# Splitting two weight blocks on VectorE, keeping key roots in PSUM, and spreading the gate columns over the last memory head

## The chip, the cores and the metric

The kernel is one program on one core of one Trainium2 chip. The metric is the device time of one execution in microseconds: a median of 1459.05 us over 3 runs (1458.96 to 1459.29). The profile shows another execution of the same program. Its engines are called PE (TensorE), DVE (VectorE), ACT (ScalarE), POOL (GpSimd) and SP (SyncE).

## The reference, cut to what matters

A two-layer encoder trunk with 512 tokens, width 1024 and a memory of 256 rows. Everything in this document happens in the first 8% of it: the keys and values that both layers read from the memory, the normed input of the first layer, and 16 "gate" columns (beta and decay of 8 heads) of the first layer's input projection.

```python
mem_n = rms_norm(mem, mem_norm[i])                 # once per layer i
mk, mv = jnp.split(mem_n @ w_mem_kv[i], 2, axis=-1)
k = rms_norm(mk.reshape(B, M, 4, 128), k_norm)     # 4 memory heads per layer
v = mv.reshape(B, M, 4, 128)
...
h = rms_norm(x, norm)
proj = h @ w_in                                    # q, k, v, z and, 8 columns each, b and a
beta = jax.nn.sigmoid(b)
g = -jnp.exp(a_log) * jax.nn.softplus(a + dt_bias)
```

After that come the gated delta rule over 8 heads, memory attention, output projection and feed-forward layer, then a second layer with sliding-window attention. None of that is touched.

## The kernel before, in words

**Precision.** Every large product is made of three: weights and activations are each split into a rounded part (`hi`) and the rest (`lo`), and PE sums hi x hi, hi x lo and lo x hi. A weight block is 128 rows by 1024 columns, that is eight 128x128 tiles, so one block is 24 matmuls.

**The weight stream.** SP loads blocks into a ring of four (`w_raw`), ACT rounds each (`upper`, writes `w_hi`, counts `hi_done`), POOL subtracts (`lower`, L563, writes `w_lo`, counts `lo_done`), and PE waits for `lo_done` before a block's first matmul (`product`, L621). SP loads block b when blocks up to b-4 have been split; ACT rounds block b when PE has used block b-4.

**Order.** Each engine runs its own fixed list, in the order in which the code is written; semaphores are the only ties. So what an engine waits for holds up everything that stands behind it in its list.

**Start.** The memory rows are scaled on ACT, transposed on PE (L641, two k-tiles share one PSUM bank), and split by ACT (`mem_upper`) and DVE (`mem_lower`), which takes four buffers' turns with it. In ACT's list the rounding of weight blocks 0 and 1 stands ahead of `mem_upper(0)`.

**Memory projections** (`mem_proj` on PE, `mem_keys` on ACT, `mem_kv` on DVE; layer 0, then layer 1). A head takes a value block and a key block, 24 matmuls of 128x256 each. DVE copies both from PSUM; PE transposes the values (L673) and sums the squared keys (`key_sums`, L651, into bank D[4]); ACT makes the root as Ln and Exp (`key_rstd`), which in the kernel before is written to the SBUF tile `w(KRS)`; DVE multiplies keys, gain and root into `kmem` (`key_normed`). The key sums of a head stand on PE after the next head's value block, those of the last head at the end.

**The input.** Between the layers PE transposes x (L683, 32 transposes for 8 k-tiles, four banks in turn) and DVE copies it to `xT`. During layer 1, `norm_rows` (L699) spreads the root of each row, and DVE and ACT make the normed tiles between the heads: `x_normed` (DVE, PSUM), `x_upper` (ACT), `x_lower` (DVE), in three banks in turn. `X_TILES` says beside which head a tile stands: 0 and 1 after the first head's keys, then one before and one after the keys of heads 1 and 2, and 6 and 7 before the keys of head 3.

**Gate columns** (L709). After layer 1, 24 matmuls of 16 columns by 512 make `ba_raw`. Then `proj_dn(0, j)`, j = 0 to 3, are the first four blocks of the input projection, with the gate chain between them: transposes (L882), exp and log on ACT, three memsets and four column copies on DVE, `conv_tile(0, 0)` (DVE adds three shifted taps, which frees the PSUM bank of block j = 0), cumulative sums (L888, L889), row matmuls (L897).

The bank names: `D = [2, 3, 4, 5, 6, 7]`.

Of the kernel before, what the change touches and what calls it, by code (L numbers as in the profile page):

```python
# [126 lines left out]
def yoco_kernel(nc, x, mem, w_stream, w_out, w_down, w_ba, cols_in, squares_in, dist_in, out):  # L127
    with ExitStack() as ctx:
# [206 lines left out]
        def w(i):  # L335
            return ws[:, i, :]
# [221 lines left out]
        def _(pool):  # L558
# [32 lines left out]
            lower_all("mem0", 8)  # L591
# [20 lines left out]
        def _(pe):  # L612
# [41 lines left out]
            def mem_proj(layer, beside=None):  # L654
                b0, n0 = BLOCK0[f"mem{layer}"], TILE0[f"mem{layer}"]
                pe.wait_ge(S.m_evac_lo, KT * (layer + 1))
                for j in range(MEM_HEADS):
# [20 lines left out]
            mem_proj(0)


            def x_transposes(k):
                for t in range(NT):
                    mm = nc.tensor.transpose(bank[:, D[k % 4], t * P:(t + 1) * P],  # L683
                                             ws[:, 2 * t:2 * t + 2, :].rearrange("p a c -> p (a c)")[
                                                 :, k * P:(k + 1) * P], sq(IDENT))
                return mm
            pe.wait_ge(S.x_loaded, 16)
            pe.wait_ge(S.m_evac_lo, 2 * KT)
# [18 lines left out]
            for k in range(KT):  # L707
                for m, (wi, at) in enumerate(((0, act_hi), (0, act_lo), (1, act_hi))):
                    mm = nc.tensor.matmul(bank[0:16, D[3], :], ba_w[:, wi, k * 16:(k + 1) * 16], at[:, k, :],  # L709
                                          start=(k == 0 and m == 0), stop=(k == KT - 1 and m == 2))  # L710
            mm.then_inc(S.ba_raw, 1)
# [536 lines left out]
        def _(act):  # L1248
# [34 lines left out]
            upper(0, 0)  # L1283
            upper(0, 1)
# [420 lines left out]
        def _(dve):  # L1705
# [546 lines left out]
```

## Time and profile before

| | |
|---|---|
| median of 3 runs | 1459.05 us (1458.96 to 1459.29) |
| the profiled execution | 1458.45 us, of which 1456.7 us are the span |
| PE busy | 1421.3 us (98% of the span), 9400 matmuls |
| PE weight loads | 1146.4 us (79%) |
| DVE, ACT, POOL busy | 38%, 40%, 38% |
| DMA | 124.15 MB, 85 GB/s mean |
| granted TensorE clock | 0.998 mean |

A row of the timeline has the start in us from the span's start, the duration in us, the engine, the line, the operation with output and inputs, the shape, how many instructions are merged, and in brackets how long the engine was idle before it and on whom it waited. Matmuls overlap: a matmul row of 0.28 us may be followed 0.12 us later by the next, so distances between starts are what counts.

### The profile page before, as it was taken

The page shows a single profiled execution, that of the slowest core. Times are in us where ns is not written, and L with a number is a line of the kernel's source. Part 1 is how long each engine was busy: PE and PEld are TensorE (multiplying, and loading weights), DVE is VectorE, ACT ScalarE, POOL GpSimd, SP SyncE. Part 2 cuts the span into 40 slices and gives each one's busy share as a digit, 9 for nine tenths or more (in the row PEclk, how much of TensorE's full clock was granted, in tenths as well). Part 3 has the DMA queues.
Part 4 walks back from the last instruction along what each step waited for, and adds up shares of the span by engine and source line. Part 5 has one row for each costly group of instructions (what it writes and reads, how often), then busy time and mean ns, then how long its engine had stood idle before and what let it go on. Part 6 is the DMA issues. An engine that isn't in the chain of part 4 may idle for free.

```text
span 1456.7 us, 24342 instructions
## 1 busy us (share of the span) xinstructions
PE 1421.3 (98%) x9400; PEld 1146.4 (79%) x9400; DVE 559.7 (38%) x1054; ACT 578.8 (40%) x989; POOL 555.0 (38%) x270
## 2 busy tenths in 40 slices
PE   6989999999999999999999999999999999999998
PEld 5867777777777888888888887777788888888887
DVE  3555666667644322220122224774322221122210
ACT  5634554454435333232322335775334232223221
POOL 4533323223321444444443444122345444433432
PEclk9999999999999999999999999999999999999999
DMA  6422111111111332323232232111232323422232
GB/s 234 131 73 88 45 59 44 45 59 59 52 45 33 105 116 87 100 80 120 91 101 92 74 115 96 59 43 50 70 115 92 110 69 99 130 84 96 73 95 78
DMA packets 39230, 124.15 MB, mean 85 GB/s; under 512 B 4192, under 2 KB 5472, under 8 KB 39136
## 3 DMA queue, kind: packets, MB, share of 16 engines
q1 hardware_dynamic: 38976, 122.55, 26.5%
q8 instruction: 69, 1.13, 0.3%
q10 hardware_dynamic: 160, 0.26, 0.1%
q14 instruction: 25, 0.20, 0.0%
HBM read 120.44 MB, written 2.10 MB: 84 GB/s over the span
## 4 chain that ended last, share of the span: by engine, by line
PE 91%; DVE 4%; ACT 2%; issue 1%; DMA 0%; DVEq 0%; SPq 0%; ACTq 0%
PE bank L621 77%; ACT ws L1250 1%; DVE ws L1718 1%; PE bank L947 1%; DVE ws L1715 1%; PE bank L818 1%; PE bank L975 1%; DVE act_lo L1715 1%; PE bank L795 1%; PE bank L1182 1%; PE bank L633 1%; PE bank L1206 1%; PE bank L864 1%; PE bank L1193 1%; PE bank L838 0%
## 5 line engine op out<-in xcount | busy, mean ns | idle before, releaser
L563 POOL TENSOR_TENSOR w_lo<-w_raw,w_hi 128x1024 fp32r<-128x1024 f32 (+1 forms) x250 | 534.0, 2152 | 772.8 <-ACT w_hi L1250 772.8
L621 PE MATMUL bank<-act_hi,w_hi 128*128 128x512 f32 (+1 forms) x1776 | 709.4, 399 | 7.5 <-DVE act_lo L1715 2.6
L621 PE MATMUL bank<-act_hi,w_lo 128*128 128x512 f32 (+1 forms) x1776 | 680.6, 383 | 0.0
L621 PE MATMUL bank<-act_lo,w_hi 128*128 128x512 f32 (+1 forms) x1776 | 680.1, 383 | 0.0
L621 PEld LDWEIGHTS bank<-act_hi,w_hi 128*128 128x128 f32 x1776 | 335.4, 189 | 75.1 <-issue 7.3
L621 PEld LDWEIGHTS bank<-act_hi,w_lo 128*128 128x128 f32 x1776 | 335.2, 189 | 65.8
L621 PEld LDWEIGHTS bank<-act_lo,w_hi 128*128 128x128 f32 x1776 | 336.0, 189 | 58.3 <-issue 2.9
L1250 ACT ACTIVATE w_hi<-w_raw 128x1024 fp32r<-128x1024 f32 (+1 forms) x250 | 230.7, 953 | 92.7 <-PE bank L621 90.6
L1709 DVE TENSOR_TENSOR ws<-bank,ws 128x512 f32<-128x512 f32 x110 | 75.9, 691 | 333.9 <-PE bank L621 323.6
L1250 ACT ACTIVATE ws<-ws 128x512 f32<-128x512 f32 (+2 forms) x128 | 83.0, 650 | 156.5 <-DVE ws L1709 111.7
L2050 DVE TENSOR_TENSOR xT<-xT,bank 128x512 f32<-128x512 f32 (+1 forms) x48 | 33.0, 687 | 258.7 <-PE bank L621 258.7
L1250 ACT ACTIVATE act_hi<-ws 128x512 fp32r<-128x512 f32 (+1 forms) x52 | 32.8, 631 | 238.1 <-DVE ws L1709 238.1
L1718 DVE COPY ws<-bank 128x512 f32<-128x512 f32 (+5 forms) x103 | 44.5, 440 | 65.7 <-PE bank L621 20.0
L1715 DVE SCALAR_TENSOR_TENSOR ws<-bank,cols,ws 128x510 f32<-128x510 f32 (+3 forms) x80 | 58.9, 736 | 13.5 <-ACT ws L1361 13.0
L1250 ACT ACTIVATE ws<-bank 128x512 f32<-128x512 f32 x49 | 29.1, 594 | 87.5 <-PE bank L1098 44.9
L1250 ACT ACTIVATE ws<-xT 128x512 f32<-128x512 f32 (+1 forms) x24 | 15.2, 632 | 107.1 <-DVE xT L2050 107.1
L1361 ACT ACTIVATE ws<-bank,cols 128x512 f32<-128x512 f32 x24 | 16.5, 686 | 98.0 <-PE bank L621 88.5
L1712 DVE TENSOR_TENSOR act_lo<-ws,act_hi 128x512 fp32r<-128x512 f32 (+1 forms) x44 | 30.5, 693 | 34.5 <-ACT act_hi L1250 34.5
L1709 DVE TENSOR_TENSOR ws<-ws 128x512 f32<-128x512 f32 x52 | 37.1, 714 | 3.1
L583 POOL TENSOR_TENSOR ws<-ws 128x512 f32<-128x512 f32 x8 | 10.2, 1280 | 59.5 <-ACT ws L1250 59.5
L1250 ACT ACTIVATE ws<-ws,st 128x128 f32<-128x128 f32 (+1 forms) x66 | 27.0, 412 | 11.7 <-DVE st L2164 11.7
L577 POOL TENSOR_TENSOR act_lo<-ws,act_hi 128x512 f32 (+1 forms) x8 | 10.9, 1365 | 52.3 <-ACT act_hi L1250 52.3
(178 smaller groups left out, 968.7 us busy)
## 6 DMA issues: line engine op xcount, KB each, us to landing
w_raw<-w_stream SPq DMA_DIRECT2D x154, 512.0 KB, 3.3
w_raw<-w_out SPq DMA_DIRECT2D x32, 384.0 KB, 3.1
w_raw<-w_down SPq DMA_DIRECT2D x32, 384.0 KB, 3.1
w_raw<-w_down SPq DMA_DIRECT2D x32, 320.0 KB, 3.1
ws<-x_in SPq DMA_DIRECT2D x1, 2048.0 KB, 8.3
ws<-mem_in SPq DMA_DIRECT2D x2, 512.0 KB, 4.5
out<-ws SPq DMA_DIRECT2D x1, 1024.0 KB, 4.2
out<-ws SPq DMA_DIRECT2D x1, 768.0 KB, 3.6
```

The costliest lines, as they stand in the source:

```text
L563: nc.gpsimd.tensor_tensor(w_lo[:, s, 0:width * P], w_raw[:, s, 0:width * P], w_hi[:, s, 0:width * P].bitcast(F32), ALU.subtract).then_inc( ...
L621: mm = nc.tensor.matmul(acc, wt[:, c % RING, wsl], at[:, act0(k0 + k), off:off + n], start=(start and k == 0 and m == 0), stop=(stop and k ...
L633: mm = nc.tensor.transpose(bank[:, dst, t * P:(t + 1) * P], tt(source, t), sq(IDENT))
L795: mm = nc.tensor.matmul(bank[quarter(q), D[3], QB * t:QB * (t + 1)], key_block(t, q, q), inverse(t, q), start=True, stop=True)
L818: mm = nc.tensor.matmul(bank[quarter(q), D[4], QB * t:QB * (t + 1)], turned(t, q), masked(t, q), start=True, stop=True)
L1250: return nc.scalar.activation(out_, in_, func, **kw)
L1361: nc.scalar.activation(w(CQ + j), psum(j % 2), ACT.Copy, scale=conv_w(h, j, 3)).then_inc(S.cv_tap, 1)
L1709: return V.tensor_tensor(out_, x_, y_, ALU.mult)
L1712: return V.tensor_tensor(out_, x_, y_, ALU.subtract)
L1715: return V.scalar_tensor_tensor(out=out_, in0=x_, scalar=scalar, in1=y_, op0=op0, op1=op1)
L1718: return V.tensor_copy(out_, x_)
L2050: V.tensor_tensor(xT[:, k, :], xT[:, k, :], psum(j), ALU.add).then_inc(S.acc_free, 1)
```

## The change

It has five parts.

1. **Blocks 0 and 1.** DVE rounds and subtracts them at the head of its list (two rounding copies, two subtractions); ACT and POOL leave them out. POOL begins with block 2 after it has waited for `lo_done` 2.
2. **Key roots.** ACT's Exp writes the root back to bank D[4], and `key_normed` reads it there. So the next `key_sums`, which writes that bank, waits for `mk_done` of the head before instead of `mk_ln`.
3. **x transposes.** They are called from inside `mem_proj(0)` in three parts: k-tile 0 ahead of the last head's value transposes, tiles 1 to 3 behind them and ahead of the last key sums, tiles 4 to 7 behind the key sums.
4. **Gate columns.** Called from inside `mem_proj(1)` in the same three places: k-tile 0, tiles 1 to 5, tiles 6 and 7, each tile behind a wait for its own `x_lower`. They accumulate in bank D[3], so the normed tiles take turns in two banks instead of three.
5. **Gate chain.** DVE's three memsets stand ahead of its wait for `ba_raw`, and `conv_tile(0, 0)` stands ahead of the four column copies.

```diff
@@ POOL
-            lower_all("mem0", 8)
+            pool.wait_ge(S.lo_done, 2)
+            for b in range(2, 8):
+                lower(0, b, KT)
@@ PE, key_sums and mem_proj
-                    pe.wait_ge(S.mk_ln, head)
+                    pe.wait_ge(S.mk_done, head)
...
+                    if j + 1 == MEM_HEADS:
+                        ahead(0)
                     pe.wait_ge(S.acc_free, n0 + 2 * j + 1)
...
                     mm.then_inc(S.mv_tr, 1)
+                ahead(1)
                 key_sums(MEM_HEADS * (layer + 1) - 1)
+                ahead(2)
...
+            def x_transposes(part):
+                if part == 0:
+                    pe.wait_ge(S.x_loaded, 16)
+                    pe.wait_ge(S.m_evac_lo, 2 * KT)
+                for k in ((0,), (1, 2, 3), range(4, KT))[part]:
+                    if due(k - 3):
+                        pe.wait_ge(S.x_raw_copied, k - 3)
...
+            mem_proj(0, ahead=x_transposes)
...
-            mem_proj(1, norm_rows)
-            pe.wait_ge(S.x_evac_lo, KT)
-            pe.wait_ge(S.ba_split, 1)
-            for k in range(KT):
...
+            def gate_columns(part):
+                if part == 0:
+                    pe.wait_ge(S.ba_split, 1)
+                for k in (range(0, 1), range(1, 6), range(6, KT))[part]:
+                    pe.wait_ge(S.x_evac_lo, k + 1)
...
+            mem_proj(1, norm_rows, gate_columns)
@@ ACT
-            upper(0, 0)
-            upper(0, 1)
             mem_upper(0)
+            act.wait_ge(S.hi_done, 2)
...
-                a(w(KRS)[:, 0:MEM_LEN], w(KRS)[:, 0:MEM_LEN], ACT.Exp, scale=-0.5).then_inc(S.mk_rstd, 1)
+                a(psum(D[4], MEM_LEN), w(KRS)[:, 0:MEM_LEN], ACT.Exp, scale=-0.5).then_inc(S.mk_rstd, 1)
...
-                a(act_hi[:, k, :], psum(D[1 + k % 3]), ACT.Copy).then_inc(S.x_evac_hi, 1)
+                a(act_hi[:, k, :], psum(D[1 + k % 2]), ACT.Copy).then_inc(S.x_evac_hi, 1)
@@ DVE
+            for b in range(2):
+                dve.wait_ge(raw_loaded[b], 16)
+                cp(w_hi[:, b, :], w_raw[:, b, :]).then_inc(S.hi_done, 1)
+            for b in range(2):
+                dve.wait_ge(S.hi_done, b + 1)
+                sub(w_lo[:, b, :], w_raw[:, b, :], w_hi[:, b, :].bitcast(F32)).then_inc(S.lo_done, 1)
...
-                stt(kmem[:, head, :], w(KR)[:, 0:MEM_LEN], col(f"mk{layer}"), w(KRS)[:, 0:MEM_LEN],
+                stt(kmem[:, head, :], w(KR)[:, 0:MEM_LEN], col(f"mk{layer}"), psum(D[4], MEM_LEN),
...
+            dve.wait_ge(S.mk_done, 2 * MEM_HEADS)
+            for i in (KBG, ZZ, TT):
+                V.memset(w(i), 0.0).then_inc(S.rw_cols, 1)
             dve.wait_ge(S.ba_raw, 1)
...
-            V.memset(w(KBG), 0.0).then_inc(S.rw_cols, 1)
-            V.memset(w(ZZ), 0.0).then_inc(S.rw_cols, 1)
-            V.memset(w(TT), 0.0).then_inc(S.rw_cols, 1)
-            dve.wait_ge(S.rw_cols, 2)
+            conv_tile(0, 0)
+            dve.wait_ge(S.rw_cols, 3)
             dve.wait_ge(S.ba_g, 1)
             for half, source in enumerate((GG, BETA)):
...
-            conv_tile(0, 0)
```

Three places of the instruction lists follow, first as they stood and then as they stand. Line numbers of the changed kernel are higher by a few: the product is L623 there, the value transposes L677, the key sums L653, the x transposes L692, the gate matmuls L713.

PE's list at the end of layer 0's memory projection, before:

```order
L621 MATMUL bank<-act_hi,w_lo 128x256
L673 MATMUL bank<-sq_c,ws 128x128 x2
L651 MATMUL bank<-ws,sq_c 128x256
L683 MATMUL bank<-sq_c,ws 128x128 x32
```

and now:

```order
L623 MATMUL bank<-act_hi,w_lo 128x256
L692 MATMUL bank<-sq_c,ws 128x128 x4
L677 MATMUL bank<-sq_c,ws 128x128 x2
L692 MATMUL bank<-sq_c,ws 128x128 x12
L653 MATMUL bank<-ws,sq_c 128x256
L692 MATMUL bank<-sq_c,ws 128x128 x16
```

Sixteen of the 32 transposes moved ahead of the last key sums, four of them ahead of the value transposes too.

PE's list at the end of layer 1's memory projection, before (24 gate matmuls L709 follow the key sums, of which the first four are shown):

```order
L621 MATMUL bank<-act_hi,w_lo 128x256
L673 MATMUL bank<-sq_c,ws 128x128 x2
L651 MATMUL bank<-ws,sq_c 128x256
L709 MATMUL bank<-act_hi,ba_w 16x512
L709 MATMUL bank<-act_lo,ba_w 16x512
L709 MATMUL bank<-act_hi,ba_w 16x512 x2
```

and now, first around the value transposes, then around the key sums (13 gate matmuls stand between the two pieces):

```order
L623 MATMUL bank<-act_hi,w_lo 128x256
L713 MATMUL bank<-act_hi,ba_w 16x512
L713 MATMUL bank<-act_lo,ba_w 16x512
L713 MATMUL bank<-act_hi,ba_w 16x512
L677 MATMUL bank<-sq_c,ws 128x128 x2
```

```order
L713 MATMUL bank<-act_hi,ba_w 16x512
L653 MATMUL bank<-ws,sq_c 128x256
L713 MATMUL bank<-act_hi,ba_w 16x512
L713 MATMUL bank<-act_lo,ba_w 16x512
L713 MATMUL bank<-act_hi,ba_w 16x512 x2
```

Eighteen gate matmuls moved ahead of the key sums, six stay behind them.

DVE's list from the last `kmem` to the end of the first convolution tile, before:

```order
L1715 SCALAR_TENSOR_TENSOR kmem<-ws,cols 128x256
L1718 COPY ws<-bank 16x512
L1824 TENSOR_TENSOR dn_s<-bank,cols 128x32
L1715 SCALAR_TENSOR_TENSOR dn_s<-dn_s 128x32
L1827 TENSOR_SCALAR dn_s<-dn_s 128x32
L1829 RECIPROCAL dn_s<-dn_s 128x32
L1835 MEMSET ws 128x512
L1836 MEMSET ws 128x512
L1837 MEMSET ws 128x512
L1718 COPY ws<-dn_s 128x4x8 x4
L1715 SCALAR_TENSOR_TENSOR ws<-bank,cols,ws 128x511
```

and now:

```order
L1720 SCALAR_TENSOR_TENSOR kmem<-ws,cols,bank 128x256
L1835 MEMSET ws 128x512 x3
L1723 COPY ws<-bank 16x512
L1839 TENSOR_TENSOR dn_s<-bank,cols 128x32
L1842 TENSOR_SCALAR dn_s<-dn_s 128x32
L1844 RECIPROCAL dn_s<-dn_s 128x32
L1720 SCALAR_TENSOR_TENSOR ws<-bank,cols,ws 128x511
L1720 SCALAR_TENSOR_TENSOR ws<-bank,cols,ws 128x510
L1720 SCALAR_TENSOR_TENSOR ws<-bank,cols,ws 128x509
L1723 COPY ws<-dn_s 128x4x8 x4
```

The memsets moved ahead of the copy of the gate rows (`16x512`), and the taps ahead of the four column copies.

## Rows read from the trace of the kernel before

**Rows 1.** The page's part 4, the chain that ended last: by engine.
```profile
PE 91%; DVE 4%; ACT 2%; issue 1%; DMA 0%; DVEq 0%; SPq 0%; ACTq 0%
```
**Rows 2.** Windows: start:end length, busy PE, PEld, DVE, ACT, POOL (instructions), clock, DMA.
```profile
17.76:23.28 5.52, 5.52 (x26) 5.52 (x27) 0.08 (x2) 2.67 (x6) 4.71 (x2) 1.00 0.54 189
...
84.13:91.79 7.66, 7.66 (x26) 3.16 (x27) 0.48 (x1) 0.89 (x2) 1.83 (x1) 0.78 0.22 71
```
**Rows 3.** DVE by form: line, operation, shapes, count | busy us, mean ns | idle before.
```profile
L1709 DVE TENSOR_TENSOR ws<-ws,st 128x1024 f32<-128x1024 f32 x8 | 9.8, 1224 | 0.3
...
L1718 DVE COPY ws<-ws 128x512 f32<-128x512 f32 x3 | 1.3, 429 | 2.1 <-ACT ws L1250 2.1
```
**Rows 4.** DMA view, the issue of block 1: KB, us from issue to landing.
```profile
w_raw<-w_stream SPq DMA_DIRECT2D x1, 512.0 KB, 7.7
```
**Rows 5.** Timeline of SP, DVE and PE, 3 to 18 us.
```profile
3.58 0.49 SPq L513 DMA_DIRECT2D w_raw<-w_stream  x1
...
15.65 2.05 DVE L1715 SCALAR_TENSOR_TENSOR act_lo<-bank,cols,act_hi 128x256 fp32r<-128x256 f32 x5 [0.37 <-ACT act_hi L1250]
...
17.76 0.58 PE L621 MATMUL bank<-act_hi,w_hi 128*128 128x256 f32 x1 [2.65 <-DVE act_lo L1715]
```
**Rows 6.** Timeline of PE and DVE at the end of layer 0's projection.
```profile
45.74 0.38 PE L673 MATMUL bank<-sq_c,ws 128*128 128x128 f32 x2
...
46.87 0.70 PE L651 MATMUL bank<-ws,sq_c 128*128 128x256 f32 x2 [0.74 <-ACT ws L1250]
47.40 1.91 PE L683 MATMUL bank<-sq_c,ws 128*128 128x128 f32 x16
...
48.97 4.86 DVE L1718 COPY xT<-bank 128x512 f32<-128x512 f32 x8
...
49.70 2.45 PE L683 MATMUL bank<-sq_c,ws 128*128 128x128 f32 x16 [0.39 <-DVE xT L1718]
...
51.91 0.36 PE L621 MATMUL bank<-act_hi,w_hi 128*128 128x256 f32 x1
```
**Rows 7.** Timeline of DVE and POOL in layer 1's projection: `kmem` and its neighbours.
```profile
62.58 2.40 POOL L563 TENSOR_TENSOR w_lo<-w_raw,w_hi 128x1024 fp32r<-128x1024 f32 x1 [2.03 <-ACT w_hi L1250]
...
63.35 1.91 DVE L1715 SCALAR_TENSOR_TENSOR kmem<-ws,cols 128x256 f32<-128x256 f32 x1 [0.74 <-ACT ws L1250]
...
67.58 2.37 POOL L563 TENSOR_TENSOR w_lo<-w_raw,w_hi 128x1024 fp32r<-128x1024 f32 x1 [2.60 <-ACT w_hi L1250]
...
69.27 0.69 DVE L1712 TENSOR_TENSOR act_lo<-bank,act_hi 128x512 fp32r<-128x512 f32 x1 [0.66 <-ACT act_hi L1250]
...
85.82 0.48 DVE L1715 SCALAR_TENSOR_TENSOR kmem<-ws,cols 128x256 f32<-128x256 f32 x1 [1.86 <-ACT ws L1250]
```
**Rows 8.** Timeline of PE and ACT in layer 1's projection: blocks 12, 13 and 15.
```profile
65.16 0.36 PE L621 MATMUL bank<-act_hi,w_hi 128*128 128x256 f32 x1
...
66.45 1.05 ACT L1250 ACTIVATE w_hi<-w_raw 128x1024 fp32r<-128x1024 f32 x1
...
68.11 0.70 PE L651 MATMUL bank<-ws,sq_c 128*128 128x256 f32 x2
70.09 0.35 PE L621 MATMUL bank<-act_hi,w_hi 128*128 128x256 f32 x1 [1.28 <-POOL w_lo L563]
...
77.77 0.35 PE L621 MATMUL bank<-act_hi,w_hi 128*128 128x256 f32 x1 [1.04 <-POOL w_lo L563]
```
**Rows 9.** Timeline of PE: last value transposes, last key sums, first input block.
```profile
80.72 0.38 PE L673 MATMUL bank<-sq_c,ws 128*128 128x128 f32 x2
84.13 0.70 PE L651 MATMUL bank<-ws,sq_c 128*128 128x256 f32 x2 [3.03 <-ACT ws L1250]
...
91.79 0.40 PE L621 MATMUL bank<-act_hi,w_hi 128*128 128x512 f32 x1
```
**Rows 10.** Timeline of ACT, DVE and PE after the gate transposes.
```profile
99.94 0.67 ACT L1361 ACTIVATE ws<-bank,cols 128x512 f32<-128x512 f32 x1
...
102.76 2.31 DVE L1715 SCALAR_TENSOR_TENSOR ws<-bank,cols,ws 128x511 f32<-128x511 f32 x3
...
103.46 0.39 PE L889 MATMUL bank<-dn_s,sq_c 128*128 128x32 f32 x2
105.12 0.50 PE L621 MATMUL bank<-act_hi,w_hi 128*128 128x512 f32 x1 [1.27 <-DVE ws L1715]
```

More of the change, by code:

```diff
@@ L649, in key_sums, with mem_proj @@
                 if due(head):
-                    pe.wait_ge(S.mk_ln, head)
+                    pe.wait_ge(S.mk_done, head)
                 nc.tensor.matmul(psum(D[4], MEM_LEN), sq(ONES), w(KS)[:, 0:MEM_LEN],
                                  start=True, stop=True).then_inc(S.mk_ss, 1)
-            def mem_proj(layer, beside=None):
+            def mem_proj(layer, beside=None, ahead=None):
                 b0, n0 = BLOCK0[f"mem{layer}"], TILE0[f"mem{layer}"]
@@ L675, in mem_proj @@
                     mm.then_inc(S.mv_tr, 1)
+                ahead(1)
                 key_sums(MEM_HEADS * (layer + 1) - 1)
[L678 to L688, printed above, removed]
-            for k in range(KT):
-                if due(k - 3):
-                    pe.wait_ge(S.x_raw_copied, k - 3)
-                x_transposes(k).then_inc(S.x_raw_tr, 1)
+                ahead(2)
[6 more added lines that the diff above has]
+                        pe.wait_ge(S.x_raw_copied, k - 3)
+                    for t in range(NT):
+                        mm = nc.tensor.transpose(bank[:, D[k % 4], t * P:(t + 1) * P],
+                                                 ws[:, 2 * t:2 * t + 2, :].rearrange("p a c -> p (a c)")[
+                                                     :, k * P:(k + 1) * P], sq(IDENT))
+                    mm.then_inc(S.x_raw_tr, 1)
+            mem_proj(0, ahead=x_transposes)
             def norm_rows():
@@ L701, in norm_rows @@
                 mm.then_inc(S.x_rows, 1)
-            mem_proj(1, norm_rows)
-            pe.wait_ge(S.x_evac_lo, KT)
-            pe.wait_ge(S.ba_split, 1)
[L707 to L711, printed above, removed]
+            def gate_columns(part):
[3 more added lines that the diff above has]
+                    pe.wait_ge(S.x_evac_lo, k + 1)
+                    for m, (wi, at) in enumerate(((0, act_hi), (0, act_lo), (1, act_hi))):
+                        mm = nc.tensor.matmul(bank[0:16, D[3], :], ba_w[:, wi, k * 16:(k + 1) * 16], at[:, k, :],
+                                              start=(k == 0 and m == 0), stop=(k == KT - 1 and m == 2))
+                if part == 2:
+                    mm.then_inc(S.ba_raw, 1)
+            mem_proj(1, norm_rows, gate_columns)
             def proj_dn(h, j, ks=range(KT)):
@@ L1297, in key_rstd @@
                 if due(head):
-                    act.wait_ge(S.mk_done, head)
+                    act.wait_ge(S.mk_rstd, head)
                 a(w(KRS)[:, 0:MEM_LEN], psum(D[4], MEM_LEN), ACT.Ln, scale=1.0 / P, bias=col("eps")).then_inc(S.mk_ln, 1)
                 act.wait_ge(S.mk_ln, head + 1)
-                a(w(KRS)[:, 0:MEM_LEN], w(KRS)[:, 0:MEM_LEN], ACT.Exp, scale=-0.5).then_inc(S.mk_rstd, 1)
+                a(psum(D[4], MEM_LEN), w(KRS)[:, 0:MEM_LEN], ACT.Exp, scale=-0.5).then_inc(S.mk_rstd, 1)
             def mem_keys(layer, beside=None):
@@ L1777, in x_normed @@
                 dve.wait_ge(S.x_raw_copied, KT)
-                if due(k - 2):
-                    dve.wait_ge(S.x_evac_lo, k - 2)
-                stt(psum(D[1 + k % 3]), xT[:, k, :], col("a_norm", k), psum(D[0]), ALU.mult, ALU.mult
+                if due(k - 1):
+                    dve.wait_ge(S.x_evac_lo, k - 1)
+                stt(psum(D[1 + k % 2]), xT[:, k, :], col("a_norm", k), psum(D[0]), ALU.mult, ALU.mult
                     ).then_inc(S.x_norm, 1)
@@ L1784, in x_lower @@
                 dve.wait_ge(S.x_evac_hi, k + 1)
-                sub(act_lo[:, k, :], psum(D[1 + k % 3]), hi(k)).then_inc(S.x_evac_lo, 1)
+                sub(act_lo[:, k, :], psum(D[1 + k % 2]), hi(k)).then_inc(S.x_evac_lo, 1)
             def x_tiles(ks):
```

## The prediction, made before the changed kernel ran

> **What bounds the kernel now.** I read the chain of waits by engine first: PE holds 91% of it, DVE and ACT share 6% [rows 1]. So the kernel is a string of PE work, and an edit pays only where it removes a wait of PE, a stretch at PE's lower clock, or PE work. The change removes no PE work (24 gate matmuls and 32 transposes are still there). I then read PE's timeline over the stretch that the diff touches, from the first product at 17.76 to the first input block at 91.79 and on to 105.12, and looked at each gap and at who ended it. There are four places. At 17.76 PE has waited for the last `mem_lower` [rows 5]. At the end of layer 0 it waits for the squared keys, then for copies of x, and goes on at 51.91 [rows 6]. In layer 1 two blocks begin late because POOL's `w_lo` is late [rows 8], and the last key sums come after 3.03 us of idling [rows 9]. Then one input block waits for the convolution taps [rows 10]. Last I read the clock: the stretch from 84.13 has a mean of 0.78 [rows 2], so part of it ran on the 1.2 GHz level, right behind the 3.03 us idle time; elsewhere up to 118 us the granted clock reads 1.00.
>
> **Part 1, blocks 0 and 1 on VectorE.** The first product waits for the memory rows, not for the weights: PE's releaser is `act_lo`, whose last five tiles run from 15.65 to 17.70 behind ACT and PE's transposes, which are not moved [rows 5]. ACT being free 2 us sooner therefore brings nothing. Can DVE be late? Block 1 is issued at 3.58 and lands 7.7 later, at 11.3 [rows 4, 5]. No row shows a rounding copy of 128x1024 on DVE. A plain copy of 512 columns from SBUF takes 0.43 [rows 3], so twice the columns take between 0.43 and 2 x 0.43 = 0.86; if rounding halves the rate, at most twice that, 1.7. I take 0.75, near the row. The subtraction is 1.22 [rows 3]. So DVE does copy 1 from 11.3 to 12.1, then two subtractions to 14.5, and needs 3 x 0.41 (2.05/5, rows 5) for the three tiles ahead of 15.65: ready at 15.7, a delay of 0.1. With the slow copy it starts 1 us later, and PE 1 us later; but the first block runs at half the usual rate anyway (26 matmuls in 5.52 [rows 2], while 24 take 68.11 - 65.16 = 2.95 in rows 8), so I count between 0 and +1, value +0.1.
>
> **Part 2, roots in PSUM.** `kmem` takes 0.48 where POOL is idle and 1.91 where a subtraction of POOL is running; in the latter case it ends at 65.26, just behind POOL's 64.98 [rows 7]. It reads two SBUF tiles. A subtraction of DVE with one operand in PSUM, in the middle of POOL's next one, keeps its 0.69 [rows 7]. So I take 0.48 for the new form; the bounds are 0.48 and 1.91. The Trainium skill (SBUF — State Buffer, "SBUF: two separate sides") says the same as a rule: DVE with two SBUF inputs and GpSimd take a shared port pair as an exclusive lock for a whole instruction. By that rule the new form never waits for POOL; without it, rival A below holds.
> What is it worth? Three heads of layer 1 have the long form. In layer 0 PE never waited for it, so nothing there. In layer 1 it stands ahead of `x_normed`, which feeds ACT's `x_upper`, which stands in ACT's list ahead of the rounding at 66.45, which feeds POOL's subtraction at 67.58 to 69.95, which ends PE's wait at 70.09 [rows 7, 8]. All of it moves 1.43 up: block 13 at 68.66 instead of 70.09. It can go no further, for the sums at 68.11 must be issued first (about 0.4). The new path into the next head: from key sums to `kmem` it takes 85.82 - 84.13 = 1.69 when nothing is in the way [rows 7, 9], so the next `kmem` starts at 68.11 + 1.69 = 69.8, and from there to PE's block it is 70.09 - 63.35 - 1.43 = 5.3: 75.1. PE alone gets there at 68.66 + 2.95 + 0.14 (two value transposes) + 2.95 + 0.4 = 75.1. So PE hardly waits any more, and block 15 begins at 75.1 instead of 77.77: -2.7. The new wait of the key sums for `mk_done` is met a whole block before.
>
> **Part 3, x transposes.** Here I see a loss. The last key sums are issued at 46.87 because the squares are ready only then. Now 16 transposes stand ahead of them. They take some 1.7 (1.91 less the overlap of the last one [rows 6]); the first follows the last product at 45.74, the two value transposes take less than two of those, 0.14, more, so the sums go at 45.74 + 1.7 + 0.14 = 47.6 to 47.7: 0.8 later. Behind the sums stand Ln, Exp and `kmem`, and only behind that the eight copies of x on DVE, 0.61 each from 48.97; DVE's list is not changed. PE's k-tile 4 needs the first copy, k-tile 7 the fourth. So copies begin at 49.8, and PE leaves for layer 1 at 52.7 instead of 51.91: +0.8, whatever PE did in the gap. Bounds: 0 (if the sums were issued as early as before) and +1.1 (each transpose at 0.12).
>
> **Part 4, gate columns.** Block 15 is issued from 75.1 to 78.05 (times without the 0.8 and 0.1). Six issues of the old order now follow without a wait: three gate matmuls, value transposes, 15 gate matmuls (all normed tiles up to 5 are long split), the key sums, six gate matmuls. Do the sums wait? They went at 84.13 because the squares were ready only then; the chain behind that moves up with block 15 and with `kmem`, 84.13 - 2.7 - 1.4 = 80.0, and PE is there at 82.4. DVE splits tiles 6 and 7 ahead of those keys, so nor do the last six wait. The price of a gate matmul is that of any 512 column one at full clock: (103.46 - 91.79)/48 = 0.24 at most [rows 9, 10]; 24 make 5.6. Sum: 78.05 + 0.14 + 5.6 + 0.4 = 84.2 for the first input block, instead of 91.79: -7.6 in all for parts 2 and 4 (2.7 of it from block 15's start, 3.3 the wait between 80.72 and 84.13, 1.6 the stretch at half clock: 7.66 - 6.0). The two banks in place of three cost nothing: each normed tile is split before the second next is made.
>
> **Part 5, the gate chain.** The memsets now run beside the first input block. The roots are done sooner than the chain, so ACT's first tap, which ended at 100.61 = 8.8 behind the input block's start, decides: three taps of 0.76 end at 102.9 instead of 105.07 [rows 10]. PE gets there at 103.46 + 0.15, so the block at 105.12 starts at 103.6: -1.5, and PE is the bound again. The four column copies (1.7) now end at 104.7, which the row matmuls 5.5 later don't feel. What follows (rows, silu, key sums at 118) hangs on PE's row matmuls, so all of it moves.
>
> **Sum.** +0.1 - 7.6 + 0.8 - 1.5 = -8.2. From there on PE is the chain, and a shift stays a shift. The profiled execution took 1458.45, so 1450.25; on the median of the runs, 1459.05, that is 1450.8.
>
> **Rivals.**
> A. The PSUM operand doesn't free `kmem` of POOL. For it: the only rows of this form beside POOL are slow. Against: its neighbour in rows 7. Then 2.7 stays away, the idle end and the clock are won all the same: -7.6 becomes -4.9, total -5.5, 1453.5.
> B. PE's clock falls at the end of layer 0. PE is idle there from about 48.2 to 50.5, longer than the 1.28 us waits that cost no clock, shorter than the 3.03 that did. For the lower level each us costs half a us; the stretch behind 84.13 cost 1.6, and the start's 5.5 us would cost 2.8. Total -8.2 + 1.6 to 2.8: 1452.4 to 1453.6. The Trainium skill (TensorE: Matmul & The Clock Gate, "What's actually happening") has it that idling, not heat, throttles PE. By that rule the transposes pulled forward make the gap behind them worse, and the sum would be B's; the row shows only that 3.03 us suffices.
> C. Slower: the clock falls in that gap and PE, which is waited for at every step of layer 1, stays at the lower level until the gate columns. From 52.7 to 84.9 some 30 us of matmuls would take twice as long: -8.2 + 30 = +22, 1481. It decides from 16 us at the lower level. Against it: the two low stretches in the trace ended after 5.5 and about 3.3 us under steady work.
> D. The loss of part 3 doesn't come, say because DVE's copies start by another release: 1450.0.
>
> **How the numbers follow.** Forecast (with D, 0.05 of it) 0.68, A 0.10, B 0.18, C 0.03, and 0.01 for something unseen. All but C are faster by more than 0.2% (2.9 us, about what one can tell from no change here); two of the losses together (A and B's upper end: 1456.3) reach into the "same", so 0.92 faster, 0.04 same, 0.04 slower. Range: 1449.3 (D, with gates at 0.22 or so each) to 1454.5 (A and B, and the slow copy of part 1).
>
> **What would show it.** `kmem` at 0.48 in all eight places; the last key sums of layer 0 about 0.8 later and block 8 at about 52.8; blocks 13 and 15 without a POOL wait over 0.3; no idle time over 1 us from there to the first input block at about 85.1; clock 1.00 through 80 to 95; the third input block within 0.2 of its predecessor's sums. The prediction is wrong if PE's first product is later than 18.3, if the clock reads under 1 between 50 and 60, or if some gap behind 105 grows by what was won.

## The result and the profile after

The changed kernel took 1451.33 us (median of 5 runs, 1450.41 to 1451.81). In the same job the kernel before took 1459.07 (5 runs, 1458.96 to 1459.67). The ratio is 0.9945, with an interval of 0.9933 to 0.9956. Run again later beside the experiments it took 1449.32 (1448.87 to 1451.58), a ratio of 0.994 [0.9927, 0.9953]. The prediction was 1450.8, within 1449.3 to 1454.5. One execution of an experiment below (part 1 undone) took 1578.32 us at a mean granted clock of 0.853 and is left out of its median and ratio.

The profiled execution took 1451.81 us, the slowest of its five, with a span of 1450.0: 6.65 less than before, where I had forecast 8.2. All of the difference is in the stretch that the diff touches. The table has the starts of six instructions on PE, read from its timeline. "Memory sums" are the last key sums of layer 0, "row sums" the first key sums of the input projection (L732 before, L738 after).

| us from the span's start | before | after | difference grows by |
|---|---|---|---|
| first product | 17.76 | 18.35 | +0.59 |
| memory sums of layer 0 | 46.87 | 48.05 | +0.59 |
| block 8, the first of layer 1 | 51.91 | 54.06 | +0.97 |
| first input block | 91.79 | 86.42 | -7.52 |
| third input block | 105.12 | 98.27 | -1.48 |
| row sums | 118.36 | 111.51 | 0 |
| end of the span | 1456.66 | 1450.01 | +0.20 |

So parts 2, 4 and 5 brought 9.0 between block 8 and the third input block, and what lies ahead of block 8 gave back 2.15. The chain of waits, by engine, of the changed kernel; PE now holds 93% of it where it held 91% [rows 1]:

```profile
PE 93%; DVE 3%; ACT 2%; issue 1%; DMA 0%; DVEq 0%; SPq 0%; ACTq 0%
```

The start, timeline of DVE, ACT and PE (start, us, engine and line, operation, shapes, count, idle time before and its releaser). It answers to [rows 5], and to the price that [rows 3] did not have:

```profile
7.98 1.06 ACT L1256 ACTIVATE ws<-ws 128x1024 f32<-128x1024 f32 x1 [2.49 <-DMA ws<-mem_in]
...
10.73 0.70 DVE L1723 CAST w_hi<-w_raw 128x1024 fp32r<-128x1024 f32 x1 [10.73 <-DMA w_raw<-w_stream]
...
14.76 1.26 DVE L1720 SCALAR_TENSOR_TENSOR act_lo<-bank,cols,act_hi 128x256 fp32r<-128x256 f32 x3
16.25 2.05 DVE L1720 SCALAR_TENSOR_TENSOR act_lo<-bank,cols,act_hi 128x256 fp32r<-128x256 f32 x5 [0.22 <-ACT act_hi L1256]
...
18.35 0.58 PE L623 MATMUL bank<-act_hi,w_hi 128*128 128x256 f32 x1 [2.65 <-DVE act_lo L1720]
```

The rounding copy on DVE takes 0.70, and DVE ends its first three `mem_lower` tiles 0.2 before ACT has the next one ready. The later start is due to the memory rows: ACT's second squaring starts at 7.98 behind a DMA (7.39 before), and from it to the first product it is 10.37 in both kernels.

The end of layer 0, timeline of PE and DVE; it answers to [rows 6]:

```profile
46.08 0.60 PE L692 MATMUL bank<-sq_c,ws 128*128 128x128 f32 x4
...
46.74 1.47 PE L692 MATMUL bank<-sq_c,ws 128*128 128x128 f32 x12
48.05 0.60 PE L653 MATMUL bank<-ws,sq_c 128*128 128x256 f32 x2
...
49.61 0.48 DVE L1720 SCALAR_TENSOR_TENSOR kmem<-ws,cols,bank 128x256 f32<-128x256 f32 x1 [2.25 <-ACT bank L1256]
50.01 5.09 DVE L1723 COPY xT<-bank 128x512 f32<-128x512 f32 x8
50.74 3.63 PE L692 MATMUL bank<-sq_c,ws 128*128 128x128 f32 x16 [2.10 <-DVE xT L1723]
54.06 0.43 PE L623 MATMUL bank<-act_hi,w_hi 128*128 128x256 f32 x1
```

The memory sums follow the last product by 1.97 instead of 1.13, PE waits 2.10 for DVE's first copy, and the second 16 transposes take 3.63 instead of 2.45. The windows (start:end, length, busy PE with its instructions, granted clock, DMA share, GB/s) say why the last is so: the clock was on the 1.2 GHz level from 50.8, just behind the wait, to 54.2. They answer to the second row of [rows 2] as the place where the clock is now lost:

```profile
50.50:51.00 0.50, 0.26 (x2) 0.80 0.02 0
51.00:51.50 0.50, 0.50 (x4) 0.50 0.00 0
...
54.00:54.50 0.50, 0.50 (x5) 0.79 0.00 0
```

Layer 1's projection, timeline of POOL, DVE and PE; it answers to [rows 7 to 9]:

```profile
70.89 0.36 PE L623 MATMUL bank<-act_hi,w_hi 128*128 128x256 f32 x1
71.03 2.40 POOL L563 TENSOR_TENSOR w_lo<-w_raw,w_hi 128x1024 fp32r<-128x1024 f32 x1 [0.28 <-ACT w_hi L1256]
71.90 0.48 DVE L1720 SCALAR_TENSOR_TENSOR kmem<-ws,cols,bank 128x256 f32<-128x256 f32 x1 [0.85 <-ACT bank L1256]
...
77.27 0.38 PE L623 MATMUL bank<-act_hi,w_hi 128*128 128x256 f32 x1
...
84.60 0.59 PE L653 MATMUL bank<-ws,sq_c 128*128 128x256 f32 x2
86.42 0.40 PE L623 MATMUL bank<-act_hi,w_hi 128*128 128x512 f32 x1
```

`kmem` keeps its 0.48 in the middle of POOL's subtraction (71.90, beside 71.03 to 73.43), where it took 1.91; all eight of them take 0.48. Blocks 13 and 15 start with no wait, and the key sums at 84.60 have none either. Behind the gate transposes, timeline of DVE and PE; it answers to [rows 10]:

```profile
86.81 1.56 DVE L1835 MEMSET ws<- 128x512 f32 x3 [0.17 <-DVE kmem L1720]
...
95.26 2.31 DVE L1720 SCALAR_TENSOR_TENSOR ws<-bank,cols,ws 128x511 f32<-128x511 f32 x3 [1.10 <-ACT ws L1366]
97.50 0.47 DVE L1723 COPY ws<-dn_s 128x32 f32<-128x32 f32 x4
...
98.27 0.48 PE L623 MATMUL bank<-act_hi,w_hi 128*128 128x512 f32 x1
```

The view of waits on PE up to 125 us (who waits <- who ends it: total us, count, longest) has two waits over 1 us beside the one for the first memory rows:

```profile
PE bank L623 <- DVE act_lo L1720: 2.6, 1, 2.6
PE bank L692 <- DVE xT L1723: 2.1, 1, 2.1
```

### The profile page after: what moved, and what is told of

It is laid out like the page before. It is cut to its first block, busy times and chain, and to the rows that moved or that the text cites. A ratio compares the mean times of both kernels' runs of the same rounds, so it can differ in the third digit from the quotient of the medians.

```text
span 1450.0 us, 24344 instructions
## 1 busy us (share of the span) xinstructions
PE 1419.7 (98%) x9400; PEld 1147.2 (79%) x9400; DVE 556.5 (38%) x1058; ACT 577.1 (40%) x987; POOL 550.8 (38%) x268
## 3 DMA queue, kind: packets, MB, share of 16 engines
q8 instruction: 69, 1.13, 0.3%
## 4 chain that ended last, share of the span: by engine, by line
PE 93%; DVE 3%; ACT 2%; issue 1%; DMA 0%; DVEq 0%; SPq 0%; ACTq 0%
PE bank L623 79%; PE bank L953 1%; ACT ws L1256 1%; PE bank L824 1%; PE bank L981 1%; DVE ws L1723 1%; DVE ws L1720 1%; DVE act_lo L1720 1%; PE bank L801 1%; PE bank L1188 1%; PE bank L635 1%; PE bank L1212 1%; PE bank L870 1%; PE bank L1199 1%; PE bank L970 0%
## 5 line engine op out<-in xcount | busy, mean ns | idle before, releaser
L623 PE MATMUL bank<-act_hi,w_hi 128*128 128x512 f32 (+1 forms) x1776 | 709.1, 399 | 3.9 <-DVE act_lo L1720 2.6
L623 PE MATMUL bank<-act_hi,w_lo 128*128 128x512 f32 (+1 forms) x1776 | 680.5, 383 | 0.0
L623 PE MATMUL bank<-act_lo,w_hi 128*128 128x512 f32 (+1 forms) x1776 | 679.8, 383 | 0.0
L623 PEld LDWEIGHTS bank<-act_hi,w_hi 128*128 128x128 f32 x1776 | 335.4, 189 | 71.3 <-issue 4.6
L623 PEld LDWEIGHTS bank<-act_hi,w_lo 128*128 128x128 f32 x1776 | 335.0, 189 | 65.6
L623 PEld LDWEIGHTS bank<-act_lo,w_hi 128*128 128x128 f32 x1776 | 335.8, 189 | 58.5 <-issue 2.9
L1256 ACT ACTIVATE ws<-ws 128x512 f32<-128x512 f32 (+2 forms) x120 | 79.7, 665 | 157.9 <-DVE ws L1714 111.8
L1256 ACT ACTIVATE ws<-bank,cols 128x512 f32<-128x512 f32 (+1 forms) x36 | 22.8, 634 | 21.3 <-PE bank L1112 8.7
```

The costliest lines, as they stand in the source:

```text
L623: mm = nc.tensor.matmul(acc, wt[:, c % RING, wsl], at[:, act0(k0 + k), off:off + n], start=(start and k == 0 and m == 0), stop=(stop and k ...
L1256: return nc.scalar.activation(out_, in_, func, **kw)
```

## The experiments

Each is the changed kernel with one edit, unless it says otherwise. A run's span carries two things that have nothing to do with the edit: ACT's second squaring started between 6.67 and 7.98 in these profiles, as the memory rows landed, and the stretch from the first product to the last product of layer 0 took 26.7 to 28.0. The second comes from the start, where products are issued 0.21 apart instead of 0.12: the four profiles with 25 to 28 such products (before, changed, five filling matmuls, all copies first and filled) took 27.7 to 28.0, the ten with 14 to 19 took 26.7 to 27.0. So I compare stretches of PE's timeline that start behind both: **a** from the end of layer 0's last product (the next issue on PE) to block 8, **b** from there to the first input block, **c** from there to the third.

| kernel | a | b | c | runs, us (before on that chip) | ratio |
|---|---|---|---|---|---|
| before | 6.17 | 39.88 | 13.33 | 1459.07 | |
| changed | 7.98 | 32.36 | 11.85 | 1451.33 (1459.07) | 0.9945 [0.9933, 0.9956] |
| changed, repeated | 6.87 | 32.28 | 11.89 | 1449.32 (1458.75) | 0.994 [0.9927, 0.9953] |
| part 1 undone | 6.87 | 32.29 | 11.89 | 1450.19 (1458.75) | 0.9943 [0.993, 0.9955] |
| part 2 undone | 6.90 | 35.03 | 11.89 | 1451.77 (1458.6) | 0.996 [0.9946, 0.9973] |
| part 3 undone | 6.13 | 32.29 | 11.90 | 1448.19 (1458.6) | 0.9939 [0.9925, 0.9952] |
| part 4 undone | 6.87 | 34.43 | 11.86 | 1453.07 (1458.62) | 0.9959 [0.9945, 0.9973] |
| part 5 undone | 6.87 | 32.28 | 13.34 | 1452.91 (1458.75) | 0.9963 [0.995, 0.9976] |
| before with part 2 alone | 6.13 | 36.02 | 13.33 | 1454.69 (1458.62) | 0.997 [0.9958, 0.9981] |
| 9 filling matmuls | 7.95 | 32.31 | 11.86 | 1451.45 (1458.6) | 0.9953 [0.9939, 0.9967] |
| 5 filling matmuls | 6.86 | 32.31 | 11.89 | 1449.13 (1458.62) | 0.9935 [0.9921, 0.9948] |
| three copies first | 5.08 | 32.30 | 11.89 | 1449.02 (1458.6) | 0.9933 [0.9919, 0.9946] |
| all copies first | 4.13 | 32.28 | 11.89 | 1446.79 (1458.62) | 0.9918 [0.9904, 0.9931] |
| all copies first, filled | 4.13 | 32.29 | 11.89 | 1446.53 (1458.75) | 0.9913 [0.9901, 0.9926] |

Where the edit and the clock leave a stretch alone it repeats to 0.1 us, the ratios only to some 0.0013, that is 2 us. What an edit of under 2 us does is therefore read from the stretches of a single profile each; the medians only fail to contradict it.

**Part 3 undone.** The 32 transposes stand behind the memory sums again.

```diff
-                for k in ((0,), (1, 2, 3), range(4, KT))[part]:
+                for k in ((), (), range(KT))[part]:
```

> The changed kernel with part 3 taken back: all 32 transposes of x stand behind the last key sums of layer 0 again. My theory: in the changed kernel the 16 transposes ahead of the sums delay them (48.05 instead of about 47.2), and so DVE's copies of x, and the idle time behind them lets PE's clock fall (0.50 from 50.8 to 54.2). Undone, the stretch from the last product of layer 0 to block 8 shrinks from 7.98 us to the 6.17 us of the kernel before, the clock reads 1.00 from 45 to 60, and the time is 1.8 us less than the changed kernel's: 1449.5. Rival 1: the clock falls at this place by chance or for another reason; then it stays at 0.50 and only 0.8 is won: 1450.5. Rival 2: the early transposes pay for the gap; then the time goes up, to about 1452.

Timeline of PE at the end of layer 0 in this kernel:

```profile
45.20 0.70 PE L653 MATMUL bank<-ws,sq_c 128*128 128x256 f32 x2 [0.75 <-ACT ws L1256]
...
48.01 2.45 PE L692 MATMUL bank<-sq_c,ws 128*128 128x128 f32 x16 [0.36 <-DVE xT L1723]
50.21 0.36 PE L623 MATMUL bank<-act_hi,w_hi 128*128 128x256 f32 x1
```

Stretch a is 6.13. That is 1.85 less than in the first profile of the changed kernel and 0.74 less than in the repeated one (6.87); the clock read 1.00. So pulling the transposes forward costs 0.7, and 1.1 more where the clock falls in the wait.

**The gap filled.** PE multiplies ones by a constant into a bank that nobody reads, after the memory sums of layer 0, first nine times, then five times.

```diff
                 key_sums(MEM_HEADS * (layer + 1) - 1)
+                if layer == 0:
+                    pe.wait_ge(S.mv_done, MEM_HEADS)
+                    for _ in range(9):       # 5 in the second kernel
+                        nc.tensor.matmul(bank[:, D[5], 0:MEM_LEN], sq(ONES), ...)
                 ahead(2)
```

> The changed kernel with nine more matmuls (128x256, constants, result unused) on PE behind the last key sums of layer 0, about 2.2 us of work in the 2.4 us in which PE was idle. It adds work and removes none. Theory: idling lets the clock fall, so it stays at 1.00 and block 8 starts 1.0 us sooner (about 53.0 instead of 54.06): 1450.3. Rival (the clock falls because transposes count as idling, or by chance): clock 0.50 as before, no gain or a small loss, 1451.3 to 1451.6.

> The changed kernel with five more matmuls of 128x256 behind the last key sums of layer 0; nine took 4.0 us and overfilled the gap, five should take 2.2. Theory: the loss in front of block 8 has two parts, DVE's copies being late (6.9 instead of 6.17 from the last product to block 8, always) and the clock (1.1 more, in executions in which it falls). Filled, the stretch is 6.9 to 7.0 and the clock reads 1.00 between the key sums and block 8, in every execution; the time is that of the better executions of the changed kernel. Rival: the stretch is 7.9 again, so the clock fall was not the cause of the last 1.1.

Timeline of PE with nine:

```profile
47.57 4.05 PE L685 MATMUL bank<-sq_c 128*128 128x256 f32 x18
...
53.12 0.36 PE L623 MATMUL bank<-act_hi,w_hi 128*128 128x256 f32 x1
```

and with five, then its window of PE behind them:

```profile
47.91 2.32 PE L685 MATMUL bank<-sq_c 128*128 128x256 f32 x10
...
52.38 0.36 PE L623 MATMUL bank<-act_hi,w_hi 128*128 128x256 f32 x1
```

```profile
50.00:53.00 3.00, 3.00 (x23) 1.00 0.00 1
```

Nine was my miscount: a filling matmul in full fp32 leaves two records and takes 0.44, so nine of them last 4.05, about 1.6 us past the copy that PE waits for. The clock stayed up, but stretch a is 7.95 by the filling itself, and this run says nothing on the clock's price. Five last 2.32 and fit: 6.86 and clock 1.00. But unfilled the same order has 6.87 in four profiles too (the repeat, and parts 1, 4 and 5 undone), so five fillings cost nothing, and that they prevent a fall isn't shown: 1449.13 against 1449.32 for the repeated changed kernel is no difference.

**The changed kernel again,** with nothing edited, to see how often the clock falls.

> The changed kernel once more, to see what scatters. If PE's clock falls in the gap behind the last key sums of layer 0 only in some executions, this profile shows either 8.0 us from the last product to block 8 with a stretch at 0.50, or 6.9 with 1.00 throughout; if the fall belongs to the kernel, it shows 8.0 again. Time 1450.4 to 1451.8.

Timeline of PE at the wait, and windows at the start and behind it:

```profile
49.19 2.45 PE L692 MATMUL bank<-sq_c,ws 128*128 128x128 f32 x16 [2.10 <-DVE xT L1723]
```

```profile
18.00:20.00 2.00, 2.00 (x11) 0.50 0.01 2
...
50.00:52.00 2.00, 2.00 (x17) 1.00 0.00 0
```

The same wait of 2.10, and this time no fall behind it. Of the six profiles that have this order and this wait (changed, repeated, parts 1, 2, 4 and 5 undone; 2.10 to 2.14) only the first has the clock at 0.50 there, and only there do the 16 transposes behind it take 3.63 instead of 2.45.

The first window is the start. There the view shows 0.50 in six profiles and 1.00 throughout in the other eight, the kernel before among them [rows 2], though products come 0.21 apart in all. In those eight the trace's record of the clock begins only with a rise, in the kernel before at 23.5, where the pace changes as well. So their 1.00 ahead of it stands for a missing record, and the pace tells the level.

**Part 2 undone.** The roots are written to SBUF again, and `kmem` reads two SBUF tiles.

```diff
-                a(psum(D[4], MEM_LEN), w(KRS)[:, 0:MEM_LEN], ACT.Exp, scale=-0.5).then_inc(S.mk_rstd, 1)
+                a(w(KRS)[:, 0:MEM_LEN], w(KRS)[:, 0:MEM_LEN], ACT.Exp, scale=-0.5).then_inc(S.mk_rstd, 1)
```

> The changed kernel with part 2 taken back: the root goes to the SBUF tile again and kmem reads two SBUF tiles. Theory: kmem takes 1.9 us again in the four places beside a subtraction of POOL, blocks 13 and 15 wait for POOL's w_lo again, and the time is 2.7 us more: 1454.0. Rival: now that PE has gate matmuls behind block 15 and the wait of the sums is filled, the stall is covered; then under 1 us more: 1452.3 or less.

Timeline of POOL, DVE and PE:

```profile
61.81 2.39 POOL L563 TENSOR_TENSOR w_lo<-w_raw,w_hi 128x1024 fp32r<-128x1024 f32 x1 [2.04 <-ACT w_hi L1256]
62.58 1.91 DVE L1720 SCALAR_TENSOR_TENSOR kmem<-ws,cols 128x256 f32<-128x256 f32 x1 [0.74 <-ACT ws L1256]
69.33 0.36 PE L623 MATMUL bank<-act_hi,w_hi 128*128 128x256 f32 x1 [1.28 <-POOL w_lo L563]
...
77.02 0.36 PE L623 MATMUL bank<-act_hi,w_hi 128*128 128x256 f32 x1 [1.07 <-POOL w_lo L563]
```

The 1.91 is back, just past the end of POOL's subtraction (64.20), and so are PE's waits of 1.28 and 1.07. Stretch b is 35.03, that is 2.7 more.

**Part 2 alone,** in the kernel before.

> The kernel before with part 2 alone (roots in PSUM). Theory: 6.2 us from the last product to block 8 as before; blocks 13 and 15 find their weights, and the last keys are squared 28.4 us after block 8 begins instead of 31.8; the first input block comes 34.4 after block 8 instead of 39.9 if the shorter idle time keeps the clock, 36.0 if not: 5.5 or 3.9 us less than before. Rival (part 2 only pays together with the moved gate matmuls): 2.7 or less.

Timeline of PE at the last sums, and a window behind it:

```profile
78.97 0.56 PE L651 MATMUL bank<-ws,sq_c 128*128 128x256 f32 x1 [1.88 <-ACT ws L1250]
```

```profile
80.00:82.00 2.00, 2.00 (x6) 0.50 0.01 2
```

Stretch b falls from 39.88 to 36.02, by 3.9: 2.7 for block 15, and 1.15 because `kmem`'s shorter form also shortens PE's wait for the last sums, from 3.03 to 1.88. The clock still fell behind it, after 1.88 us.

**Part 4 undone.** All gate columns behind the last key sums again.

```diff
-                for k in (range(0, 1), range(1, 6), range(6, KT))[part]:
+                for k in ((), (), range(KT))[part]:
```

> The changed kernel with part 4 taken back: all 24 gate matmuls stand behind the last key sums. Theory: PE idles again until the last keys are squared, 28.4 us after block 8 begins, and then needs 6.0: 34.4 from block 8 to the first input block instead of 32.4, so 2.0 us more, 1453.4; if the idle time of about 2.1 us lets the clock fall, 1.6 more on top. Rival: the last squares come sooner without the gate matmuls beside them, and under 1 us is lost.

Timeline of PE:

```profile
77.76 0.38 PE L677 MATMUL bank<-sq_c,ws 128*128 128x128 f32 x2
80.02 0.70 PE L653 MATMUL bank<-ws,sq_c 128*128 128x256 f32 x2 [1.88 <-ACT ws L1256]
```

The same wait as with part 2 alone, 1.88, but the clock stayed at 1.00, and stretch b is 34.43, 2.1 more than with part 4. So part 4 hides that wait, and spares the lower clock where this would follow: 36.02 against 34.43 is 1.6.

**Parts 1 and 5 undone.** ACT and POOL split blocks 0 and 1 again; and the memsets stand behind the gate chain again and the first convolution tile behind the four column copies.

```diff
-            pool.wait_ge(S.lo_done, 2)
-            for b in range(2, 8):
-                lower(0, b, KT)
+            lower_all("mem0", 8)
```

> The changed kernel with part 1 taken back: ACT and POOL split blocks 0 and 1 again. Theory: PE's first product hangs on the memory rows, so from ACT's second squaring of the memory rows to the first product it stays 10.37 us as in all runs so far, and the time is that of the changed kernel within its scatter (1450 to 1452). Rival: the early split saves something behind the first product (block 4's load starts sooner); then the stretch from the first product to the end of layer 0 is longer here than the 26.8 to 27.7 us with part 1.

> The changed kernel with part 5 taken back: memsets and column copies ahead of the first convolution tile. Theory: the third input block comes 13.3 us behind the first again instead of 11.9, so 1.5 us more: 1452.8. Rival: with the gate rows copied sooner than before the chain is ahead and part of it is hidden; then 12.8 or less.

Timeline of PE with part 1 undone, the first product:

```profile
17.96 0.38 PE L621 MATMUL bank<-act_hi,w_hi 128*128 128x256 f32 x1 [2.65 <-DVE act_lo L1720]
```

The first product stands 10.37 behind ACT's second squaring, as in the changed kernel and the one before. The distance isn't the same in all runs: it is 10.23 in the repeat and with part 4 undone, and 10.05 with part 2 alone, which has no part 1. So part 1 is worth nothing that stands out of this scatter, up or down. It has no room left either: with part 5 undone the memory rows came soonest (6.67), and DVE ran its eight `mem_lower` tiles without a gap, from 13.64 to 16.99, with the first product again 10.37 behind. Part 5 undone, timeline of DVE, POOL and PE:

```profile
91.33 2.40 POOL L563 TENSOR_TENSOR w_lo<-w_raw,w_hi 128x1024 fp32r<-128x1024 f32 x1 [10.39 <-ACT w_hi L1256]
92.40 1.66 DVE L1723 COPY ws<-dn_s 128x32 f32<-128x32 f32 x4
96.34 0.50 PE L623 MATMUL bank<-act_hi,w_hi 128*128 128x512 f32 x1 [1.28 <-DVE ws L1720]
```

The wait of 1.28 is back, and stretch c is 13.34, 1.45 more.

**DVE's copies first.** The loss of part 3 sits in DVE's list: `kmem` waits for ACT, and the copies that PE waits for stand behind it although the first transpose is ready some 3 us before. So three copies, and in a second kernel all eight, go ahead of layer 0's last `kmem`; ACT rounds block 10 ahead of the squares of x, so that it isn't held behind them, and in the second kernel ahead of the last key root too. These are two edits in each kernel, and the runs don't separate them.

```diff
+                if layer == 0:
+                    x_raw_copies(range(3))   # range(KT) in the second kernel
                 key_normed(MEM_HEADS * (layer + 1) - 1)
```

> The changed kernel with two lists reordered: DVE makes the first three copies of x ahead of the last kmem of layer 0 (it idled there for 2.25 us), and ACT rounds block 10 ahead of the squares of x. Theory: copies start at about 47.3 instead of 50.0, the seventh k-tile is transposed 2.9 us sooner, the clock stays at 1.00, block 8 starts at about 51.2 instead of 54.06, and block 10 finds its weights ready: 1448.4. Rival: something else gives the start of block 10 or of norm_rows (ACT's roots of x end only at about 56.7), and the gain is cut to 1 us or less: over 1450.3.

> A version meant to beat both. The changed kernel, with all eight copies of x on DVE ahead of the last kmem of layer 0, and ACT's rounding of block 10 in the 1.5 us in which ACT waits for the last key sums. From the last product of layer 0 to block 8 it is 5.08 us with three copies ahead; now nothing but PE and the copies counts, so I expect 4.4. From block 8 to the first input block 32.3 as in the last runs, if norm_rows finds the roots of x (they end 1.05 sooner than with the rounding in front of the squares). Time: 2.5 us less than the changed kernel where its clock doesn't fall, 3.6 less where it does. Rival: norm_rows or block 10 waits, and what is won ahead of block 8 comes back behind it (b8 to input block over 32.8).

Timeline of DVE with three copies first, then of DVE and PE with all of them:

```profile
46.01 1.88 DVE L1725 COPY xT<-bank 128x512 f32<-128x512 f32 x3
...
48.74 3.08 DVE L1725 COPY xT<-bank 128x512 f32<-128x512 f32 x5
```

```profile
45.98 4.86 DVE L1726 COPY xT<-bank 128x512 f32<-128x512 f32 x8
...
48.91 0.36 PE L623 MATMUL bank<-act_hi,w_hi 128*128 128x256 f32 x1
50.76 0.47 DVE L1723 SCALAR_TENSOR_TENSOR kmem<-ws,cols,bank 128x256 f32<-128x256 f32 x1
```

Stretch a is 5.08 and 4.13: with all eight first the whole of PE's wait is gone, and with it the place where the clock could fall. Counted from the last product, `kmem` is 2.5 later than in the repeated kernel (5.98 instead of 3.52 behind it), and nobody feels it, for b stays at 32.28. At 0.9918 this beats the changed kernel; on the same chip its five runs (1446.41 to 1447.79) all lie below those of the five fillings (1448.85 to 1450.35).

Its profile with three copies had the lower clock at another place, in the second layer, where PE waits about 2.3 us. Window of PE there:

```profile
886.00:888.00 2.00, 2.00 (x5) 0.50 0.00 0
```

From the row sums to the end of the span that run took 1339.99, the changed kernel 1338.50. It was the same with parts 4 and 5 undone and with part 2 alone (1339.8 to 1340.1); the other ten profiles have no fall there and 1338.2 to 1338.8, nine of them with the same wait. So the last kernel puts two filling matmuls there as well.

```diff
+            for _ in range(2):
+                nc.tensor.matmul(bank[:, D[5], :], sq(ONES), ...)
             pe.wait_ge(S.kv_sq, 1)
```

> The best version so far with two more matmuls of 128x512 (constants, result unused) in PE's 2.3 us wait in the second layer's key projection, 880 us in, where three of ten traces show the clock at 0.50 for 3.4 us. Theory: the filler keeps the clock at 1.00 there, the part of the span behind the first delta head's key sums is 1338.2 to 1338.7 in every profile instead of 1340.0 in some, and the time is 0.5 us less on the median and scatters less: 1446.3. Rival: the filler delays the sums behind it, or the scatter comes from elsewhere: 1446.8 or more.

Timeline of PE:

```profile
884.32 1.12 PE L1161 MATMUL bank<-ws,sq_c 128*128 128x512 f32 x2 [0.59 <-ACT ws L1259]
```

PE's wait shrinks from 2.3 to 0.59, and the clock stays at 1.00 in this profile. The time, 0.9913 [0.9901, 0.9926], can't be told from the version without it, whose own profile had no fall either. It is the best ratio measured here; that the filling earns part of it isn't shown.

## Why the prediction was right

**Part 1** (forecast +0.1, within 0 to 1): 0 within a scatter of 0.3. The rounding copy took 0.70, near the 0.75 chosen; the slow bound of 1.7 was not met. The first product was behind 18.3, which I had named as a sign that the prediction is wrong, but it was the memory rows' landing that moved it, not DVE. The sign was badly chosen: it should have been the distance from ACT's second squaring.

**Part 2** (0.48; block 15 earlier by 2.7): `kmem` is 0.48 beside POOL, and undoing it costs 2.7. The undone kernel runs rival A's case: 2.7 stays away, as priced. With the root in PSUM none of it does, so A is refuted. The rule quoted from the Trainium skill (SBUF — State Buffer, "SBUF: two separate sides") agrees with these rows: 1.91 with two SBUF operands, ending 0.3 behind POOL's instruction, 0.48 with one in PSUM.

**Part 3** (+0.8): the undone kernel and the repeated one differ by 0.74. The sums' 0.8 delay is passed through `kmem` to the copies and to PE, as worked out.

**Part 4 with part 2** (-7.6): 32.28 against 39.88 in the undisturbed profiles, so -7.60. The split of it into 2.7, 3.3 and 1.6 needs care: part 2 alone brings 3.9, because a shorter `kmem` shortens the last wait too; from there part 4 brings 2.1, and 1.6 more where the clock had fallen.

**Part 5** (-1.5): -1.44, by 13.33 and 11.89; undoing it gives 13.34.

In stretches a to c, the repeated profile differs from before by +0.70 - 7.60 - 1.44 = -8.34, with -8.3 forecast for parts 2 to 5. What the first profile has more is rival B, to which I had given 0.18: the clock fell in the gap of 2.10, and stretch a took 1.11 longer than in the repeat. I had priced it at 1.6 to 2.8, too high: 3.4 us at the lower level, but in part of it PE would have waited for DVE's copies at 0.61 each anyway (argued from the rows; no run separates it). Rival C, that the clock stays low through layer 1, didn't happen: it was on its way back at 54.0. B and C both take the start for a stretch at the lower level although [rows 2] shows 1.00 for it; the pace bears that out. Two of the three signs that I had named for a wrong prediction were thus met in the first profile: the first product at 18.35, and the clock at 0.50 between 50.8 and 54.2. The second is rival B and no fault of the sum, but the forecast gave it only 0.18, from one row at 3.03. The range was also narrower than my own terms: A and B together with the slow copy make 1450.8 + 2.7 + 1.6 + 0.9 = 1456.0 at least, not 1454.5. Neither A nor the slow copy came, so it wasn't put to the test.

The mechanisms of parts 2 to 5 are borne out by the stretches. That the first median comes so near is in part luck: its profile fell 1.55 short of the forecast 8.2, of which 1.11 is rival B and 0.59 the later memory rows. The median of the first job lies 0.5 above the forecast; that of the repeat lies 1.2 below its own kernel before less 8.2 (1458.75 - 8.2 = 1450.55). Both are within what the landing of the memory rows (6.67 to 7.98) and the clock move from run to run; of this scatter only the clock in one gap was in the prediction, and neither the rows' landing nor the length of the slow start.

## What to carry to other kernels

Before work is pulled forward on one engine, look at who reads it: here PE's first 16 transposes came 1.7 us sooner, but DVE's list still had the copies behind an instruction that waits for the very sums which the transposes delayed. Moving the consumer's half as well turned a loss of 0.7 into a gain of 2 (stretch a: 6.17, 6.87 and 4.13). And where DVE stalls beside POOL, see whether one operand can be left in PSUM: here it cost nothing that the traces show and took 1.4 us off a chain three times. It ties the bank for longer: the next key sums wait until `kmem` has read it.

## What the hardware showed that I had not expected

**The same wait lowers the clock in one execution and not in another.** A wait of 2.10 on PE was followed by a fall in one profile of six; 1.88 was in one kernel (part 2 alone) and not in another (part 4 undone); 2.3 in the second layer was in four profiles of thirteen; 3.03 was in the kernel before. The price was 1.1 behind the 2.10, 1.6 behind the 1.88, and some 1.5 in the second layer (1339.8 to 1340.1 against 1338.2 to 1338.8). The Trainium skill (TensorE: Matmul & The Clock Gate, "What's actually happening") has idling as the cause, and every fall seen here stands behind idle time of PE: behind these waits, behind the one for the first product, or where PE has run out of work at the end. But what decides it in a given execution stays open.

**Small SBUF copies are held by POOL too.** The four column copies of 128x32 took 1.77 before (101.07 to 102.84, beside POOL's 100.11 to 102.51) and 1.66 with part 5 undone, and end about 0.3 past POOL's subtraction in both. Behind POOL's subtraction, as the changed order has them, they take 0.47. I had carried 1.7 for them into the new order. With part 2 alone they take 1.77 beside POOL again. They have one input only, so what POOL holds up isn't limited to instructions that read two SBUF tiles. The misjudged 1.7 cost nothing, since PE reads these columns much later.
